# Head norms of q and k: a power on GpSimd in place of a root on ScalarE and a reciprocal on VectorE

## What is computed

```python
def _rms(x, g):
    y = x * lax.rsqrt(jnp.mean(x * x, axis=-1, keepdims=True) + RMS_EPS)
    return y * g
fq = _rms(fq.reshape(n_b, n_t, 8, 64), fq_g)                # also fk
dq = _rope(_rms(dq.reshape(n_b, n_t, 4, 2, 64), dq_g), pos)  # also dk
```

## Time and profile before

| | us |
|---|---|
| three runs | 1354.49 median, 1353.02 to 1355.77 |
| the profiled execution | 1354.91 |
| its span, first to last instruction | 1353.0 |
| mean granted TensorE clock | 0.945 of full speed |
| busy: PE, DVE, ACT, POOL | 1288.7, 377.3, 209.9, 145.0 |

### The profile page before, as it was taken

The page is one execution under the profiler, slowest core; times in us unless marked ns, Lnnn a source line. Parts: engine busy times, 40 slices in busy tenths (PEclk is TensorE's granted clock), DMA queues, the critical chain, the costliest instruction groups (busy, mean ns, idle before and its releaser), DMA issues.

```text
span 1353.0 us, 16150 instructions
## 1 busy us (share of the span) xinstructions
PE 1288.7 (95%) x6083; PEld 573.3 (42%) x6084; DVE 377.3 (28%) x958; ACT 209.9 (16%) x524; POOL 145.0 (11%) x340
## 2 busy tenths in 40 slices
PE   6799999999998999999999999999999999999997
PEld 3344444565454433434344343443434344343432
DVE  3213223557252322213222121311212132121212
ACT  5111322346150101101001010100101010010100
POOL 0021300000004101011010110101011010101000
PEclk9899965579998999999999999999999999999998
DMA  8901440036525999999999999999999999999994
GB/s 286 323 29 74 174 168 1 0 128 226 209 70 210 431 427 427 428 429 429 428 430 428 428 429 429 428 428 430 428 428 430 428 429 428 430 428 427 429 426 183
DMA packets 54537, 447.06 MB, mean 330 GB/s; under 512 B 10817, under 2 KB 11090, under 8 KB 29922
## 3 DMA queue, kind: packets, MB, share of 16 engines
q1 hardware_dynamic: 54498, 446.54, 79.4%
HBM read 441.66 MB, written 4.86 MB: 330 GB/s over the span
## 4 chain that ended last, share of the span: by engine, by line
PE 65%; DMA 25%; SPq 4%; DVE 2%; POOL 1%; issue 1%; ACT 1%; DVEq 0%; POOLq 0%; ACTq 0%
DMA arena<-in_w_gate_up 23%; PE psum L1588 17%; PE psum L1556 16%; PE psum L1537 7%; PE psum L1303 5%; PE psum L1451 3%; PE psum L1407 3%; PE psum L1603 2%; PE psum L1359 2%; SPq L390 2%; PE psum L1387 1%; PE psum L1339 1%; PE psum L1571 1%; PE psum L1567 1%; PE psum L1355 1%; SPq L406 1%
## 5 line engine op out<-in xcount | busy, mean ns | idle before, releaser
L1556 PE MATMUL psum<-arena 128*64 128x512 f32 x2048 | 450.5, 599 | 18.9 <-DMA arena<-in_w_gate_up 18.4
L1556 PEld LDWEIGHTS psum<-arena 128*64 128x64 f32 x2048 | 152.9, 138 | 314.7 <-issue 314.7
L1588 PE MATMUL psum<-arena 128*64 128x512 f32 x1024 | 224.8, 597 | 0.8
L1210 DVE TENSOR_SCALAR arena<-psum 128x256 f32<-128x256 f32 x64 | 26.7, 418 | 432.4 <-PE psum L1556 430.6
L1588 PEld LDWEIGHTS psum<-arena 128*64 128x64 f32 x1024 | 78.8, 138 | 136.0 <-issue 134.6
L1303 PE MATMUL psum<-arena 128*128 128x512 f32 x288 | 127.6, 599 | 0.0
L838 ACT ACTIVATE arena<-arena 128x256 f32<-128x256 f32 x64 | 26.7, 418 | 630.5 <-DVE arena L1210 630.5
L1537 PEld LDWEIGHTS psum<-arena 128*128 128x128 f32 x768 | 88.5, 194 | 16.1 <-issue 16.1
L1537 PE MATMUL psum<-arena 128*128 128x128 f32 x768 | 91.6, 279 | 3.8 <-POOL arena L604 3.8
L1603 PE MATMUL psum<-arena 128*128 128x512 f32 x192 | 93.2, 623 | 0.0
L597 POOL COPY arena<-arena 128x6 f32 (+1 forms) x16 | 3.0, 188 | 775.6 <-PE psum L1588 703.5
(11 more groups left out here) (215 smaller groups left out, 905.2 us busy)
## 6 DMA issues: line engine op xcount, KB each, us to landing
arena<-in_w_gate_up SPq DMA_DIRECT2D x128, 2048.0 KB, 25.0
arena<-in_w_down SPq DMA_DIRECT2D x64, 2048.0 KB, 22.6
arena<-in_w_in SPq DMA_DIRECT2D x6, 2048.0 KB, 19.6
arena<-in_cache_fox_k SPq DMA_DIRECT2D x8, 512.0 KB, 3.5
arena<-in_cache_diff_k SPq DMA_DIRECT2D x8, 512.0 KB, 4.4
arena<-in_cache_fox_v SPq DMA_DIRECT2D x8, 512.0 KB, 4.0
arena<-in_cache_diff_v SPq DMA_DIRECT2D x8, 512.0 KB, 5.6
arena<-in_w_out SPq DMA_DIRECT2D x4, 1024.0 KB, 7.5
```

Source lines behind the costliest of these rows:

```text
L1556: last = mm(banks[n][half], XT[u][:, k, half], piece_slot(s[x])[:, c0:c0 + 512], start=False, stop=(k == 7), skip_group_check=True)
L1588: last = mm(banks[hf][half], actT[:, 4 * i + c, half], w, start=False, stop=(i == 1 and c == 3), skip_group_check=True)
```

## The change

The root on ACT and the reciprocal on DVE go. POOL raises the mean to the power -0.5 in one instruction. The exponent is a column of `stat`, filled once with -0.5 and read as 8 equal columns. The wait for `z_rt` on DVE stays, and POOL signals it now. POOL's loop now goes over all q and k units, those without rotary too, so that the power of a unit stands behind the rotary of the unit before it. The wait for the rotary's tables (`s_rot`) comes behind the power.

```diff
@@ POOL
-            g_.wait_ge(s_rot, 16)
+            g_.wait_ge(gain_ready, 1)
+            nc.gpsimd.memset(stat[:, 44:45], -0.5).then_inc(half_ready, 1)
+            g_.wait_ge(half_ready, 1)
             for u, (bi, kind, g, t) in enumerate(units):
-                if kind == "v" or g == 0:
+                if kind == "v":
                     continue
                 n = TILES[t][1]
+                rw = rows_of(u)
+                g_.wait_ge(z_ms, upto(is_n, u) + 1)
+                nc.gpsimd.tensor_tensor(ss8[rw, 1], ss8[rw, 0], stat[rw, 44:45].to_broadcast([n, 8]), ALU.pow
+                                        ).then_inc(z_rt, 1)
+                if g == 0:
+                    continue
+                g_.wait_ge(s_rot, 16)
                 o = upto(is_o, u)
-                rw = rows_of(u)
@@ ACT
                     nc.scalar.activation(sq[rw], z, ACT.Square).then_inc(z_sq, 1)
-                    ac.wait_ge(z_ms, m + 1)
-                    nc.scalar.activation(ss8[rw, 1], ss8[rw, 0], ACT.Sqrt).then_inc(z_rt, 1)
                     late.append(u)
@@ DVE
                 ve.wait_ge(z_rt, m + 1)
-                link(nc.vector.reciprocal(ss8[rw, 1], ss8[rw, 1]))
```

More of the change, by code:

```diff
@@ L232, in build @@
         z_scaled, z_T, zT_copied, ff_done = sem("z_scaled"), sem("z_T"), sem("zT_copied"), sem("ff_done")
+        half_ready = sem("half_ready")
         gain_ready, zero_ready, meta_v = sem("gain_ready"), sem("zero_ready"), sem("meta_v")
```

## The result

The changed kernel takes 1359.76 us (median of 6 runs, 1359.03 to 1362.09); the kernel before took 1354.14 beside it (6 runs). The ratio is 1.0045, 95% interval 1.0034 to 1.0057: 4.6 to 7.7 us slower. The profiled execution took 1362.03 us, its span is 1360.2.

The account below looks back on a forecast made before the run. PE bounds the projections and attention, and DMA weight streaming the experts, carrying earlier losses to the end. Four places at +0.45 us sum to +1.8 us on the 1354.49 median: 1356.3 us, range 1353 to 1363.

Parts of the forecast that it names:

- the four places: Units 6, 8 and 12, where PE already stalls on the rotary, and unit 17 before the attention: +0.45 us each.
- the dear power: Rival: a power of 1.08 to 3.5 us slows the same four units and unit 13; 1361 at 2 us; chance 0.36.
- The price of the power: One 128x8 power on Pool, assumed 0.85 us from 40 steps a column, bounds 0.2 and 1.9.
- p: Duration of one power on Pool, taken as 0.85 us; each norm then changes by p - 0.40 us.
- the plain units: q and k units without rotary (0 to 2, 9 to 11, 15): the longer norm costs nothing there.
- Pool's queue: A unit's power stands behind the previous unit's rotary on Pool: free up to p = 1.7, then unit 13 adds p - 1.7.
- the power of unit 15: At unit 15, a unit without rotary in the projections: its longer norm was to cost nothing.
- ScalarE, freed: ScalarE, no longer waiting for the mean, starts its next copies about 1 us sooner; it feeds nothing PE waited for.
- The two table loads: ScalarE's loads at the root and ahead of the exponential: first goes, second may; both hidden, any win capped at 0.12 us.
- The last place: Unit 17, whose norm, rotary and store lead to the first exponential: +0.45 us.
- its cap of 0.12 us: At unit 17 before the attention, PE's own scores limit any win to 0.12 us.
- The clock: Rival: PE's half-speed piece in the attention shifts against the work and gains 2.7 us or more; chance 0.07.

Follow-up runs that it names:

- e5: The kernel before, with powers of 1 to 32 columns and a product of 8 added on idle Pool at the start; one execution of 1355.13 us.
- e3: Against the kernel before: power on Pool only for the units without rotary (0 to 2, 9 to 11, 15); 1355.14 us, ratio 1.0005.
- e4: Against the kernel before: power on Pool only for the rotary units 6 to 8 and 12 to 14; 1357.52 us, ratio 1.0034.
- e11: Against the kernel before: power on Pool for unit 17 alone, root and reciprocal elsewhere; 1356.59 us, ratio 1.0011.
- e2: The changed kernel with a product in place of the power; routing changes, so its 1932.97 us says nothing; stretch from unit 6's square to first exponential 94.85 us.
- e9: The changed kernel with a product by 1 in place of the power; routing changes, so its 1690.73 us says nothing; unit 6's square to first exponential 94.66 us.
- e1: The changed kernel with a second power of the same size ahead of each power; 1370.27 us, ratio 1.0131 to the kernel before.
- e7: The kernel before (root and reciprocal) with one of the rotary's products moved from Pool to DVE's second product; 1352.40 us, ratio 0.9984.
- e6: The changed kernel (power) with the rotary's two products that go to rb moved from Pool to DVE; 1357.05 us, ratio 1.0007 to the kernel before.
- e8: As e7, with SP's loads of the decode caches and cached forget gates issued behind the stores of units 0 to 2; 1340.59 us, ratio 0.9890 to before.
- e10: The changed kernel with SP's loads of the caches issued behind the stores of units 0 to 2; 1350.36 us, ratio 0.9967 to the kernel before.

## Why the prediction came out as it did

The direction, slower, and the four places were right, and the time lies within the range of 1353 to 1363. The forecast itself, 1356.3 and no measurable difference, was wrong. It is the second case, the dear power, that came true.

**The price of the power.** This is the term that was mis-sized: 0.85 us was taken, 1.64 was measured. The bounds of 0.2 and 1.9 held, but the point between them was an assumption on the number of steps, 40. At 2.1 ns a step and column the measured 157 ns a column are 75, and the fixed part is 0.4 us, not 0.19 (e5). With p = 1.64 the prediction's own sum is 4 x 1.24 = 5.0 us, against 5.6 by the medians.

**Where it counts.** Shown: the stalls grew by 3.60 us in all, 3 x 1.24 being 3.72, and the gap at unit 17 by 1.24. e3 shows the plain units free in their sum (unit 15 below), e4 and e11 the two parts by themselves, e2 and e9 that nothing is lost without the power's length. e1 shows it in proportion.

**Pool's queue.** It was said to cost nothing up to p = 1.7. At 1.64 it is at that edge. Unit 7's rotary ends at 101.62 and its turn starts at 101.68, behind unit 8's matmuls and not overlapped with them as at 100.79 before; with unit 13 and the hand-overs that is about 0.36 us in the stretch beyond the stalls. In e1, past the edge, units 7 and 13 wait openly. Not foreseen is what the power of unit 15, priced at nothing, does. It does not wait for unit 14's rotary:

```profile
158.04 0.74 POOL L573 TENSOR_TENSOR arena<-arena 128x256 f32<-128x256 f32 x1
158.93 1.64 POOL L556 TENSOR_TENSOR arena<-arena 16x8 f32<-16x8 f32 x1
```

The mean is ready at 158.85, after the rotary's end at 158.78. But the power's own 1.24 us makes the store later. It is issued at 162.02 and not at 157.29, 3.48 us of which the stalls ahead had cost already, and it comes that much closer to the next store: 3.45 us ahead of it and not 4.71. The load of w_out between the two probably runs into that store, which lands 4.89 us after its issue. ACT then waits 1.98 us for a `zo` buffer and PE 0.64 ahead of unit 21. That it is unit 15's power is shown: e3, with this power and root and reciprocal at unit 14, has the wait (0.61), and e4, the other way round, has not. In the changed kernel the two ways to the scores end together, PE's at 186.4 and the exponential's reading at 186.3. So the 0.64 us adds next to nothing to what unit 17 costs anyway.

**ScalarE, freed.** It was said to feed nothing that PE waited for. That held up to unit 21: there PE waits 0.64 us for ACT's copy of unit 18 (L721), since ACT meets a wait that was hidden before, the one for the `zo` buffer. So this step failed, without a price in this kernel.

**The two table loads.** Both went, without gain, as said.

**The last place.** The changed kernel won nothing there, so its cap of 0.12 us was not put to the test; e7 did that, and the cap fell: it held at half clock alone. A gain bounded by PE's own work has to be reckoned at both of its clocks.

**The clock.** It was the rival for a gain, and brought none. Of the 2.35 us behind the exponential 0.78 lie ahead of the experts and 1.57 in them. Over the traces of before, the changed kernel, e1, e3, e4, e6, e7, e8, e10 and e11 the first part takes 238.6 to 241.2 us and the second 932.0 to 934.7, in no order that follows the powers. Whether a part of the 2.35 belongs to the change is open.

## What to carry to other kernels

Removing two cheap instructions and a hand-over wins no more than the time between their neighbours, here 0.50 us; so the question is what the one that replaces them costs, and where the trace does not show it, a few microseconds of an idle engine measure it. Count a latency at the places where something waits for it, and look at the cheapest way to shorten the same chain: here sharing the rotary took away stalls that faster norms could hardly touch. And look first at the longest idle time of the bound engine; its 8.2 us had nothing to do with the norms.

No run here shows a power on DVE, which would save both hand-overs.

## What the runs showed of the hardware

- A power on GpSimd costs 157 ns for each column and some 0.4 us beside, 75 times a product's 2.1 ns a column (e5, 1 to 32 columns, and the earlier trace rows); 16 partitions cost as much as 128 (1.63 against 1.64 us, changed kernel).
- Products on DVE and GpSimd at once, each with two inputs in SBUF (the on-chip memory), are slower, and unevenly: DVE's took 1.50 us where its neighbour of the same size took 0.43, Pool's 1.46 in place of 1.27 (e6, all six full units).
